# Seven products of quarters for the prompt rows of a down projection, and a hand-over of two half-matrix sums from GpSimd to VectorE

## The reference

```python
up  = rmsnorm(x, g_ffn_pre) @ ffn_w_up              # 1024 -> 2 * 2816 channels
ext = concatenate([conv_hist, up], axis=1)
c   = ffn_conv_b + sum(ext[:, j:j+T] * ffn_conv_w[j] for j in range(3))
act = gelu(c[..., :2816], approximate=True) * c[..., 2816:]
x   = x + rmsnorm(act @ ffn_w_down, g_ffn_post)     # down projection: 2816 -> 1024
```

## Time and profile before

| what | value |
|---|---|
| the profiled execution: its time, its span | 1567.42 us, 1565.7 us |
| TensorE busy | 1524.1 us (97% of the span) |
| VectorE busy | 898.4 us (57%) |
| ScalarE busy | 583.8 us (37%) |
| GpSimd busy | 300.0 us (19%) |
| mean granted TensorE clock | 0.982 |

### The profile page before, as it was taken

How to read it: one execution, slowest core, us unless ns; L and a number is a source line. 1 busy time by engine, 2 the same in 40 slices (tenths; PEclk the granted TensorE clock), 3 DMA queues, 4 the chain that set the end, 5 groups by cost and what they waited for, 6 DMA issues and landing times.

```text
span 1565.7 us, 26850 instructions
## 1 busy us (share of the span) xinstructions
PE 1524.1 (97%) x10067; PEld 1415.8 (90%) x10067; DVE 898.4 (57%) x1545; ACT 583.8 (37%) x1084; POOL 300.0 (19%) x293
## 2 busy tenths in 40 slices
PE   7999999999999999999997999999999999999997
PEld 7889999989999999997877999999999998788875
DVE  6575465657332233226558777777777775554644
ACT  7233132333222122114445444444444444453432
POOL 1124133340100000000124333333333320000000
PEclk9999999999999899999998999999999999999999
DMA  7234455451332432304114666655662138665471
GB/s 259 59 109 132 142 174 173 141 173 35 112 113 69 121 110 67 121 14 135 71 45 125 218 218 199 219 191 188 220 221 83 64 111 300 226 216 177 157 243 66
DMA packets 145809, 227.65 MB, mean 145 GB/s; under 512 B 14011, under 2 KB 116441, under 8 KB 144831
## 3 DMA queue, kind: packets, MB, share of 16 engines
q1 hardware_dynamic: 136711, 203.97, 40.8%
q0 software_dynamic: 8736, 22.08, 3.8%
q10 hardware_dynamic: 288, 0.59, 0.1%
HBM read 196.46 MB, written 74.34 MB: 173 GB/s over the span
## 4 chain that ended last, share of the span: by engine, by line
PE 91%; DVE 4%; DMA 2%; ACT 1%; issue 1%; SPq 0%; ACTq 0%; DVEq 0%
PE PS L1323 28%; PE PS L1144 19%; PE PS L1389 13%; PE PS L1039 9%; PE PS L1282 6%; PE PS L1020 4%; PE PS L1208 2%; PE PS L1096 2%; PE PS L1068 1%; PE PS L1384 1%; PE PS L1082 1%; PE PS L1252 1%; PE PS L1001 1%; DMA as_stage<-acts 1%; PE PS L1052 1%
## 5 line engine op out<-in xcount | busy, mean ns | idle before, releaser
L1323 PE MATMUL PS<-h_lo,wr_hi 128*128 128x264 f32 x1056 | 216.7, 286 | 0.0
L1323 PEld LDWEIGHTS PS<-h_lo,wr_hi 128*128 128x128 f32 x1056 | 165.6, 190 | 0.0
L1323 PE MATMUL PS<-t_hi,wr_hi 128*128 128x264 f32 x704 | 149.9, 292 | 7.6 <-DVE h_lo L2296 4.1
L2334 DVE TENSOR_TENSOR wd_lo<-wd_stage,wd_hi 128x1024 fp32r<-128x1024 f32 x66 | 80.8, 1224 | 118.3 <-ACT as_hi L1762 118.2
L1323 PE MATMUL PS<-h_hi,wr_hi 128*128 128x264 f32 x704 | 145.5, 288 | 0.7 <-DVE cext L2362 0.5
L1323 PE MATMUL PS<-t_hi,wr_lo 128*128 128x264 f32 x704 | 145.3, 286 | 0.0
L2020 DVE TENSOR_TENSOR tw_lo<-tw_stage,tw_hi 128x1024 fp32r<-128x1024 f32 (+1 forms) x28 | 32.6, 1166 | 177.7 <-ACT tw_hi L1533 177.5
L1323 PEld LDWEIGHTS PS<-t_hi,wr_hi 128*128 128x128 f32 x704 | 110.8, 191 | 9.1 <-DVE h_lo L2296 4.7
L1761 ACT ACTIVATE wd_hi<-wd_stage 128x1024 fp32r<-128x1024 f32 x66 | 69.8, 1057 | 130.9 <-PE PS L1389 76.6
L1144 PE MATMUL PS<-hT_hi,tw_hi 128*128 128x352 f32 x480 | 111.2, 342 | 1.8 <-issue 1.8
L1323 PEld LDWEIGHTS PS<-h_hi,wr_hi 128*128 128x128 f32 x704 | 108.9, 189 | 3.5 <-DVE wr_lo L2286 0.7
(11 more groups left out here) (317 smaller groups left out, 3444.3 us busy)
## 6 DMA issues: line engine op xcount, KB each, us to landing
wd_stage<-in_ffn_w_down SPq DMA_DIRECT2D x66, 512.0 KB, 3.6
tw_stage<-in_ffn_w_up SPq DMA_DIRECT2D x88, 256.0 KB, 4.8
out_k_s<-in_cache_k_w SPq DMA_DIRECT2D x8, 2044.0 KB
out_v_s<-in_cache_v_w SPq DMA_DIRECT2D x8, 2044.0 KB
qb<-zs SPq DMA_DIRECT2D x24, 512.0 KB, 5.1
acts<-cact POOLq DMA_DIRECT2D x22, 528.0 KB, 9.4
tw_stage<-in_w_in SPq DMA_DIRECT2D x20, 512.0 KB, 5.3
as_stage<-acts SPq DMA_DIRECT2D x44, 192.0 KB, 3.9
```

The costliest lines, as they stand in the source:

```text
L1323: last = pe.matmul(PS[:, bank + b, 0:BH], w[slot][:, k, :], x[:, k, b * BH:(b + 1) * BH], start=(k == 0 and j == 0), stop=(k == HK - 1 and ...
L2334: dve.tensor_tensor(wd_lo[slot][:, :], wd_stage[slot][:, :], wd_hi[slot][:, :].bitcast(F32), ALU.subtract)
```

## The change

Down projection: the activations' 2816 channels are cut in two halves (11 k-blocks each), the 1024 prompt rows in two, the 1024 output channels in two. Seven products of quarters, in the order 1, 2, 6, 7, 4, 5, 3, each of 11 slots (k) by 4 row tiles by 3 passes of 512 columns, take the place of eight. The sample rows keep full products: riding on the slots of products 1 and 2 (low output half) and in 11 short slots of their own (product "0", high output half), 88 matmuls of 512 columns as before. A slot has a 128x512 weight and a 128x512 activation; both are split as before through a ring of four (seven for the last three slots). The weights stay in SBUF after one load (`dw`), and the activations of each slot are staged in four buffers `ds`. Ten sums per k (T1, S1, T4a, S2, T2, S3, T3, T4b, Sa, Sb), each of 128x512, are DVE's, two slots ahead of their use; each waits for the sum before it. Products are gathered in `C1` and `C2`: ACT copies product 1 out of PSUM, DVE adds the others when it stands at slot 1 of the next product.

```diff
+        PRODUCTS = (1, 2, 6, 7, 4, 5, 3)
+        for k in range(HK2):
+            for at_, c in ((max(AT[1, k] + 2, 3), "T1"), (AT[2, k], "S1"), (AT[2, k] + 1, "T4a"), (AT[6, k] - 2, "S2"), (AT[6, k] - 2, "T2"),
+                           (AT[7, k] - 2, "S3"), (AT[7, k] - 2, "T3"), (AT[4, k] - 2, "T4b"),
+                           (AT[5, 2 * k + 2] if k < 4 else AT[3, k] - 2, "Sa"), (AT[5, 2 * k + 2] if k < 4 else AT[3, k] - 2, "Sb")):
+                SUMS_AT.setdefault(at_, []).append((c, k))
...
             sp.wait_ge(p_done, 7 * FC + U0)
+            load_down((1, 4))
+            load_down((1, 5))
+            sp.wait_ge(cnat_out, 32 * FC)
+            load_down((1, 6))
+            load_s(0)
+            load_down((1, 7))
...
+            load_smp(1)
+            load_down((1, 8))
...
+            def load_down(x):
+                n, k = x
+                u = STAGE[x]
+                st, signal = ds[u % 4], wd_in[u % 4]
+                if u >= 4:
+                    sp.wait_ge(wd_lo_done, AT[STAGED[u - 4]] + 1)
...
             def split_down(x):
...
+                if AT[x] == 3:
+                    act.wait_ge(act_ready, FC)
...
+                elif AT[x] >= 4:
+                    act.wait_ge(wd_used, AT[x] - 3)
+                w, a = operands(x)
+                act.activation(dw_hi[r][:, :], w, ACT.Copy)
+                act.activation(da_hi[r][:, :], a, ACT.Copy).then_inc(wd_hi_done, 1)
...
             near(FC - 1, 0)
-            low_down(3)
             far(FC - 1, 0)
             gated_up(FC // 2 - 1, 1)
...
+            dve.wait_ge(cnat_done, FC)
+            for x in SLOTS[3:]:
+                for c, k in SUMS_AT.get(AT[x], ()):
+                    down_sum(c, k)
+                low_down(x)
...
+                if k == 1 and n in PRODUCTS[2:]:
...
+                    for i in range(4):
+                        evict(PRODUCTS[PRODUCTS.index(n) - 1], i)
+                if x == (3, 2):
+                    fold()
...
+                if n == 3 and k >= 5 and k < 9:
+                    finish(k - 5)
+            finish(4)
+            evict(3, 0)
+            for i in range(5, NTILE):
+                if i < NTILE - 1:
+                    evict(3, i - 4)
+                finish(i)
```

```diff
@@ gpsimd
             low_t(1, 2, 0)
-            second_half(HALF_TILES[3])
-            second_half(HALF_TILES[4])
-            low_t(3, 4, 0)
-            low_t(7, 4, 1)
@@ vector
-            summed(0, 0, 2, 2)
+            second_half(HALF_TILES[3])
+            summed(0, 0, 3, 3)
             low_t(2, 3, 0)
-            summed(0, 0, 3, 3)
             out_turned(8)
-            dve.wait_ge(t_sums, TS0 + 6)
+            second_half(HALF_TILES[4])
+            dve.wait_ge(t_lo_done, U0 + 3)
             low_t(5, 2, 1)
             low_t(6, 3, 1)
+            low_t(3, 4, 0)
+            low_t(7, 4, 1)
             low_t(4, 1, 0)
             low_t(8, 1, 1)
```

More of the change, by code:

```diff
@@ new lines, in build @@
+        PRODUCTS = (1, 2, 6, 7, 4, 5, 3)
+        SLOTS = []
+        for n in PRODUCTS:
+            for k in range(HK2):
+                SLOTS.append((n, k))
+                if n == 4 and k % 2:
+                    SLOTS.append((0, k // 2))
+                if n == 5 and k % 2 == 0:
+                    SLOTS.append((0, 5 + k // 2))
+        AT = {x: i for i, x in enumerate(SLOTS)}
+        STAGED = [x for x in SLOTS if x[0] not in (0, 5)]
+        STAGE = {x: i for i, x in enumerate(STAGED)}
@@ new lines, in _, with load_row @@
+            sp.wait_ge(w_lo, 7 * FC + U0 + 1)
+            load_smp(1)
+            load_down((1, 8))
+            load_down((1, 9))
+            load_s(1)
+            load_down((1, 10))
+            load_down((2, 0))
+            sp.wait_ge(c_out, 7 * FC + U0)
+            load_s(2)
+            def load_row(i):
+                n = FINAL[i]
+                t0, rows = tile_of(n)
+                if i >= 2:
+                    sp.wait_ge(y_ready, i - 1)
+                else:
+                    sp.wait_ge(wd_lo_done, AT[3, 0])
+                sp.dma_start(xrow[i % 2][0:rows, :], x2s[t0:t0 + rows, :]).then_inc(wq_in[1][i % 2], 16)
@@ L801, in store_y @@
             def store_y(i):
-                n = DOWN_ORDER[i]
+                n = FINAL[i]
                 sp.wait_ge(y_ready, i + 1)
[L804 to L817, removed]
@@ L821, in _ @@
+            for i in range(NTILE):
+                store_y(i)
+                if i + 2 < NTILE:
+                    load_row(i + 2)
             for s in range(3):
@@ new lines, in tile_part, with sample_part @@
+            def tile_part(x, i):
+                n, k = x
+                r, bank = ring(x), (4 * PRODUCTS.index(n) + i) % 6
+                for j, (a, w) in enumerate(((da_hi, dw_hi), (da_hi, dw_lo), (da_lo, dw_hi))):
+                    mm = pe.matmul(PS[:, bank, :], a[r][:, i * P:(i + 1) * P], w[r][:, :],
+                                   start=(k == 0 and j == 0), stop=(k == HK2 - 1 and j == 2))
+                return mm
+            def sample_part(bank, f, w_hi_, w_lo_, first, last):
+                passes = ((2 * TS, w_hi_), (TS, w_lo_))
+                for j, (both, w) in enumerate(passes[::-1] if last else passes):
+                    mm = pe.matmul(PS[0:both, bank, :], smp_d[f // HK2][:, f % HK2, 0:both], w[:, :],
+                                   start=(first and j == 0), stop=(last and j == 1))
+                return mm
@@ new lines, in square @@
+            def square(i):
+                n = FINAL[i]
+                rows = tile_of(n)[1]
+                if n == 8:
+                    act.wait_ge(t_step, U0 + 12)
+                    act.wait_ge(wd_lo_done, AT[5, 0] + 1)
+                else:
+                    act.wait_ge(f_free, freed_at(5 if n >= 4 else 3, n % 4))
+                act.activation(in_halves(fjunk[0:rows, :]), finished(n), ACT.Square, accum_out=pss[0:rows, 1, n:n + 1]).then_inc(o_ss, 1)
+                act.wait_ge(o_ss, 9 + i + 1)
+                act.activation(prms[0:rows, 1, n:n + 1], pss[0:rows, 1, n:n + 1], ACT.Sqrt, bias=eps[0:rows, 0:1],
+                               scale=1.0 / D).then_inc(o_rms, 1)
@@ new lines, in _ @@
+            for s_, x in enumerate(SLOTS[3:], 3):
+                split_down(x)
+                if x == (1, 6):
+                    split_smp(1)
+                if x == (2, 1):
+                    act.wait_ge(act_out[1], 16 * (FC // 2))
+                    act.wait_ge(wd_used, AT[1, HK2 - 1] + 1)
+                    for i in range(4):
+                        act.activation(C1[:, i, 512:D], PS[:, i, :], ACT.Copy).then_inc(u_out, 1)
+                if x[0] == 3 and 3 <= x[1] < 8:
+                    square(x[1] - 3)
@@ L1852, in _ @@
+            for i in range(5, NTILE):
+                square(i)
         @block.vector
```

440 lines of the change are left out of this document (278 added, 162 removed).

## The result

The changed kernel takes **1575.08 us** (median of 5 runs, 1574.5 to 1578.35) against 1566.67: ratio 1.0057, 95% interval 1.0043 to 1.0070, so it is **slower by 0.6%**. The forecast was 1563.1 with a range of 1554.5 to 1573.5: wrong in sign, and outside the range. The profiled execution took 1574.5 (span 1572.8), 7.1 us more than the profiled one of before, where the sum said 3.6 less.

The account below looks back on a forecast made before the run. It took TensorE's matmuls to bound the down stage, the rest hidden. Terms -30.0 - 1.1 + 9.0 + 2.1 + 14.5 + 4.2 - 2.3 gave -3.6 us, so 1563.1 for the median, range 1554.5 to 1573.5.

Parts of the forecast that it names:

- 1, matmuls: Down projection: 924 full-tile matmuls instead of 1056, 30.0 us less, and the old ring's one stall gone, 1.1 less.
- Part 3: Hand-over into product 1: waits for the last `gated_up` and sample rows, plus half clock, 9.0 us more (4.3 to 14).
- Part 4: Four-buffer staging loop: product 6 loses nothing, product 7 some 8 slots x 0.33 less lead, 2.1 us more.
- Parts 5 and 6: Product 3 and the tail after it: VectorE has all at once, 14.5 us more, then 4.2 more after the last matmul.
- Part 7: Transition to up: VectorE's `low_t` no longer run beside POOL's, so `c11` comes earlier, 2.3 us less (0 to 4).
- Less half a us of lead: Staging loop, product 7: deduction from the loss of some 8 slots x 0.33, leaving 2.1 us.
- Rival B: Staging buffers bind in products 6 and 7 if landings take 4.8 us: slower, 1573.2 us; chance 0.17.
- Rival D: Transition gains nothing, VectorE's longer queue taking what POOL's absence gives: 1565.4 us, no change; chance 0.08.
- The wait for `gated_up`: Product 1, slot 3: its splits wait for the last `gated_up`, so TensorE waits 4.3 us.
- The one for the sample rows: Product 1, slot 7: ScalarE waits for the late-loaded sample rows, so TensorE waits 3.6 us.
- Rival A: Hand-over costs only the wait for `gated_up`, loads landing in time: 4.7 us less, 1558.4 us; chance 0.20.
- Rival C: VectorE starts operations 0.69 us apart, even those that wait for nothing: 1568.9 us, no change; chance 0.07.

Follow-up runs that it names:

- e1: Changed kernel with the two sums of a slot in products 6 and 7 made one slot ahead instead of two: 1564.12 us.
- e8: e6 and e7 together, plus the third weight sum's low part and the last tile's transposes put back in the transition: 1550.11 us.
- e12: Kernel before with only the change's transition, the third weight sum's low part and last tile's transposes put back: 1564.71 us, ratio 0.9992.
- e2: Changed kernel with nine of eleven pairs of product 3's sums made in product 5, stored in dS instead of a staging buffer: 1570.20 us.
- e6: Changed kernel with the edits of e1 and e2, and product 3's evictions, finishes, squares, sample copy and row buffers rearranged: 1553.71 us.
- e7: Changed kernel with the fourth operand buffer moved to memory free earlier and product 1's weight sums six slots behind its splits: 1574.27 us.

## Why the prediction was wrong

The terms beside what the runs show, in us against the kernel before (the last line is the sum of the lines, next to the measured difference of the two profiled executions):

| part | forecast | measured |
|---|---|---|
| 1, matmuls | -31.1 | -31.4 |
| 3, hand-over (products 1 and 2) | +9.0 | +8.0 |
| 4, staging loop (products 6 and 7) | +2.1 | +8.9 |
| 5 and 6, last product and tail | +18.7 | +21.4 |
| 7, transition | -2.3 | -0.6 |
| sum | -3.6 | +6.3 (profiled: +7.1) |

**Part 4 is the step that failed**, and it alone turns the sign. Its price of the bare loop was nearly right: the prediction gave "6.1, 3.05 per slot" for product 7, and the starts at 1419.38 and 1425.36 are 5.98 apart. Ten of product 7's eleven loads landed in 3.2 to 3.4 us, under the 3.5 taken; one took 4.58, and no run shows why. What the prediction left out is that the four evictions of the product before, started 0.79 us apart, 3.07 together, stand on VectorE inside the same loop; it counted evictions only in part 5. "Product 6 (256 KB): 5.2 for two, under 5.44, nothing lost" left TensorE 0.24 us of slack per two slots, 1.3 in the product. But the slot that holds the evictions took 5.53 (1406.53 to 1412.06 above; 5.52 in product 6), 2.8 more than TensorE's 2.72. VectorE could not make that up: with the waits for loads the slots behind it took 2.77 in product 6 (1378.58 to 1397.99, seven slots) and 3.13 in product 7 (1412.06 to 1433.97, seven), where its operations alone need 2.53 (a slot of e1, 1373.60 to 1376.13). The one load of 4.58 is some 1.3 of that. "Less half a us of lead" was wrong too: VectorE came late out of the product before each time, so the evictions held banks (waits of 1.2 and 1.5 us for L2634 and L2636). e1 shows the cause, by one slot more for a load and no operation less: with it both products take 29.9 although the evictions are still there. What the evictions gave by themselves is read from the trace; no run took them alone out of the loop.

Rival B named the mechanism, and TensorE's idling in product 6, its sign, is there. That its time, 1573.2, lies near the measured one is in part luck: it asked for landings over 4.5 us in every slot and priced 12.2 us for the two products, where 8.9 were lost at landings of 2.6 and 3.3 with that one exception, and parts 5 to 7 made up the rest.

**Part 7 failed as well.** The six `low_t` alone took 7.04 us (832.31 to 839.35), 7.1 forecast. But the prediction looked only at what stops overlapping with GpSimd, and not at what the new order puts there: the sum's low part, 2.95 us instead of 0.67, and behind it the last tile's row, its transposes and its splits. So `c11` ended at 841.25 and not near 838.5. e8 and e12, which put back that one step and the transposes, give 2.85 less than before, where the forecast was 2.3. Rival D's time for the transition was closer, for another reason than it gave.

**Parts 5 and 6** were right in kind (VectorE binds from product 5 to the last store: e2, e6) and short by 2.7. The last `lo` was done 39.4 us after product 5 instead of 37.5, waits for residual rows and staging among it. Then came a term that the prediction had only in the hand-over: from there to its last matmul TensorE took 8.9 us instead of 6.8, at half clock at first. Part of that came back in the tail, 8.8 instead of 10.1.

**Part 3** has the right size with only half of its reasons in sight, so the agreement is in part luck. The wait for `gated_up` was 3.95 us (4.3 forecast), as TensorE's timeline has it:

```profile
1310.20 0.79 PE L1494 MATMUL PS<-dw_hi,da_hi 128*128 128x512 f32 x1 [3.95 <-DVE da_lo L2498]
```

The one for the sample rows, 3.6 forecast, did not appear, since slot 3 had already stopped TensorE that long; half clock (7 matmuls, 1.5), a wait for the last `c12` (1.0 with its restart) and one for ScalarE's copies (1.0) filled its place. e7 shows the second wait as soon as the first is gone. The two were added, but they overlap: a wait behind another counts only for what it exceeds. Rival A's sign, no idle time at slot 7, was there, and yet the part cost 8.0 and not A's 4.3.

**Rival C** falls. In product 7 the two splits of a slot start 0.61 and 0.60 us after the operation before them (1420.11, 1420.72, 1421.32 above), and a sum, which waits for the sum before it, 0.73 after that one (1419.38, 1420.11), each lasting 0.68 or 0.69. The Trainium skill, page "VectorE: DVE Perf Modes", section "The DRAIN you can't avoid", says both that the next operation doesn't start until the pipe is empty and that one that is not held starts earlier; the trace agrees with the second sentence.

## What to carry to other kernels

Price a loop over buffers with everything that its engine does in it, the evictions of the neighbouring product too, and compare the sum with the slack of the whole product, not the loop alone with one slot. When sums are made ahead of use, each slot of lead is taken from the time that a load has: one slot less lead was worth 9 us here. On an engine that has become the bound, order the work by who waits for it: two evictions, all splits, then the finishes, with one 1.2 us copy given to ScalarE, took 10.6 us off product 3 and 6.8 off the stage.

## What the runs showed of the hardware

GpSimd beside VectorE: a 128x512 operation on VectorE with both operands in SBUF, started 0.6 us after GpSimd's 3.01 us operation, ended 0.55 us after that one's end and so took 2.95 instead of 0.67; in e12 an operation that reads one operand from PSUM and one from SBUF took 0.67 during GpSimd's (820.63 above). The Trainium skill, page "SBUF — State Buffer", section "SBUF: two separate sides", says that VectorE operations with two SBUF inputs and GpSimd operations hold a shared pair of ports one at a time; the trace agrees, in both directions of the test. By that rule the new place of the sum's low part could have been priced beforehand, by an estimate of the rest of GpSimd's operation and its own 0.6.

Half clock came back late in the kernel, after VectorE's pace had broken up TensorE's work: some 22 matmuls in product 3 of the changed kernel started 0.43 us apart, which cost 4.8 us in all, behind waits of 1.97, 2.04 and 2.77 us; the granted clock of the product was 0.86. In product 3 of e6, where no wait is longer than 0.43 us, there are none, and the granted clock was 1.00.
